# Loads of small tables issued inside the phase before, and the last projection stores no longer waited for

## Chip, cores and metric

One core of a Trainium2 chip. The metric is the device time of one execution in microseconds; the time before is the median of three runs.

## The reference, cut to what matters

A small network over 256 latent and 256 context tokens of width 1024: two layers with adaptive normalisation (adaln), then a block with a router and 32 experts. Layer 0 mixes neighbourhood attention and a bidirectional mLSTM; layer 1 is an RWKV-7 mixer; block 2 mixes a gated delta rule and a state-space scan. What the change touches is how their small parameters come on chip: norm gains, gate biases, rope and mask tables, the decay tables w2 and a2, the rows k_a and r_k, the router's bias. The computation is not changed.

```python
def modulate(x, shift, scale):
    return rms_norm(x) * (1.0 + scale) + shift
...
    r, k, v = jnp.einsum('sbtd,sde->sbte', jnp.stack([xr, xk, xv]), w_rkv)
    w_logit = w0[:, None, None, :] + jnp.einsum('zbtr,zrd->zbtd', jnp.tanh(jnp.einsum('btd,zdr->zbtr', xw, w1)), w2)
    decay = jnp.exp(-jnp.exp(-jax.nn.softplus(-w_logit.astype(jnp.float32)) - 0.5))
    a = jax.nn.sigmoid(a0[:, None, None, :] + jnp.einsum('zbtr,zrd->zbtd', jnp.einsum('btd,zdr->zbtr', xa, a1), a2))
...
    k_dir = k[None] * (1.0 + (a - 1.0) * k_a)
...
    s = s * wt[:, :, None, :] + sa[..., None] * bt[:, :, None, :] + vt[..., None] * kt[:, :, None, :]
```

## The kernel before

The kernel is a chain of phases. A Phase (from L131) owns semaphores and buffers; at its end it clears the semaphores and puts a barrier over all engines (L157), so no engine begins the next phase before all have ended this one. Inside a phase each engine has its own program, and they meet on semaphores.

Weights come through a ring of three slots of 2 MB (class Ring). SP issues a ring load (L219) when the matmuls of the chunk that used the slot are done, and it runs up to three slots ahead, so that the first three weight chunks of the next stage are under way when a phase ends. All of SP's loads go through one queue, the ring's and the small ones; ScalarE's stores of the projection go through another.

Small tables come through load (L3375), a phase of its own: SP issues all loads of the list (L3384), waits for all of them, and the barrier follows. There are nine such phases: ldx (const 1280 KB, x 4 x 512 KB) at the very start; ldab (gate_b, qn, kn, rope; 328 KB) between norm0a and the projection of layer 0; ldsel (sel 8 KB, head_row 256 KB) before mlstm_rows; ldrw (w2 512, a2 512, masks 673, ka 512, rk 512 KB) between rw_project and the scan rw_chunks; ldro (v 2 x 512, lnx_w 512, lnx_b 512, g2 512 and 128 KB) between gate_rows and rw_readout; ldgain (8 KB) between adaln and norm_T of block 2; ldconv (taps 72, cbias 18, small2 32 KB) before gd_conv; ldmix (gn 64, sn 512 KB) before gd_merge; ldmoe (router_b 16, iota 512 KB) before the router.

Phases that the change touches:
- adaln (L416): twelve chunks of 2 MB of ada_w through the ring, each multiplied by the silu of the condition (L481), copied out by ScalarE (L450), turned (L470) and added to the bias on VectorE (L461).
- gate_rows (L489): VectorE spreads gate columns (L503), TensorE turns them (L517), VectorE copies them out (L507).
- norm_T (L522): squares on ScalarE (L550), scale on VectorE (L561), normalised rows (L572), turned by TensorE (L586), written to xT by VectorE (L542).
- mlstm_rows (L1028): scans over gate rows on VectorE alone.
- rw_project (L1410): 20 units of k, v, r; VectorE copies each to one of three stage buffers, ScalarE stores it to a scratch tensor in HBM (L1570). At the end ScalarE waits for all stores, those of k times k_k (kk) too.
- rw_chunks (L1676): eight steps of a scan; SP loads k, kk, r (L1735) and v (L1740) for each; the first matmuls are logits (L1774 with the bias rows, L1775 with w2 and a2); mix_k (L2117) uses ka, k and kk; bonus uses rk from the third step on.
- gd_merge (L2780), where VectorE uses gn and sn after a root by ScalarE.

Of the kernel before, what the change touches and what calls it, by code (L numbers as in the profile page):

```python
# [13 lines left out]
ALU = mybir.AluOpType  # L14
# [3 lines left out]
P = 128  # L18
# [219 lines left out]

class G:
# [176 lines left out]
def adaln(g, name, cond, bias, mod):  # L416
# [3 lines left out]
    with Phase(g, name) as ph:  # L420
# [33 lines left out]

# [34 lines left out]
def gate_rows(g, name, cols, rows):  # L489
# [3 lines left out]
    with Phase(g, name) as ph:  # L493
# [3 lines left out]
        with nc.Block() as block:  # L497
            @block.vector
# [23 lines left out]
def norm_T(g, name, tiles, dst, scale, shift, gain=None, off=0):  # L522
# [4 lines left out]
    with Phase(g, name) as ph:  # L527
# [8 lines left out]
        with nc.Block() as block:  # L536
            def drain(dve, i):
# [490 lines left out]
def mlstm_rows(g, rowg, rowo, cols):  # L1028
# [4 lines left out]
    with Phase(g, "mlrows") as ph:  # L1033
# [4 lines left out]
        with nc.Block() as block:  # L1038
            @block.vector
# [370 lines left out]
def rw_project(g, mu, krow, lora_w, bias_rows, scr, low_w, low_a, sg0, sg1, b16, pick, loads):  # L1410

    nc, ring = g.nc, g.ring
    DEPTH, BANKS, STAGES = 7, 4, 3
# [5 lines left out]
    with Phase(g, "rwproj") as ph:  # L1419
# [4 lines left out]
        stage = ph.sb("stage", [P, STAGES, 512])  # L1424
        kkb = ph.sb("kk", [P, 2, 512])
# [17 lines left out]
        s_st = [ph.sem(f"stored_{i}") for i in range(STAGES)]  # L1443
# [4 lines left out]
        with nc.Block() as block:  # L1448
# [11 lines left out]
            def _(pool):  # L1460
# [20 lines left out]
                def finish(u):  # L1481
                    pool.wait_ge(s_ri, u + 1)
                    o = kkb[:, u % 2, :]
                    v.tensor_tensor(heads8(o), heads8(o), rep(ss[:, 2, 8 * u:8 * u + 8], RW_D, 2), ALU.mult).then_inc(s_kk, 1)

                for u in range(KK_UNITS):
# [4 lines left out]
                    v.tensor_tensor(kkb[:, u % 2, :], stage[:, u % STAGES, :], krow[:, c * 512:c * 512 + 512], ALU.mult)\  # L1491
# [45 lines left out]
            def _(act):  # L1537
# [5 lines left out]
                def square(u):  # L1543
# [3 lines left out]
                    nc.scalar.activation(sq[:, 0:512], kkb[:, u % 2, :], ACT.Square).then_inc(s_sq, 1)  # L1547
# [128 lines left out]
def rw_chunks(g, scr, low_w, low_a, w2, a2, ctab, b16, pick, rows, y, coef):  # L1676
# [3 lines left out]
    with Phase(g, "rwkv") as ph:  # L1680
# [2035 lines left out]
```

## Time and profile before

| | |
|---|---|
| runs | 3873.45, 3879.27, 3878.82 us; median 3878.82 |
| profiled execution | 3875.51 us, span 3873.7 |
| TensorE busy | 3174.9 us (82%) |
| VectorE / ScalarE / GpSimd busy | 1503.0 / 889.4 / 308.0 us |
| mean granted TensorE clock | 0.905 of full |
| data moved | 684.76 MB, 177 GB/s over the span |
| expert stage | about the last 1100 us, one expert in every 32 us |

Shares over the span say little here, since stages with different limits follow one another. The order of time and the holes between phases are read from the timeline.

### The profile page before, as it was taken

Reading aid. Unit: us, or ns where it says so; the run is one execution under the profiler, and the core shown is the slowest. Engines: PE = TensorE matmul, PEld = TensorE weight load, DVE = VectorE, ACT = ScalarE, POOL = GpSimd, SP = SyncE. Lnnn points to the kernel's source line nnn. Section 1 sums busy time; section 2 is a strip of 40 time slices with the busy share of each in tenths; the row PEclk is TensorE's granted clock in tenths of the full one; section 3 lists DMA queues with packets and bytes.
Section 4 is the critical chain, followed back from the end, with each engine's and each line's share of the span. In section 5 each row is a group of like instructions: output and inputs, shape, how many; then the busy total and the mean of one; then the engine's idle time right before and its main releaser. Section 6 shows DMA issues by size and latency. Waiting matters only on the chain. (4 is left out here: it accounts for less than half of the span.)

```text
span 3873.7 us, 94421 instructions
## 1 busy us (share of the span) xinstructions
PE 3174.9 (82%) x41870; PEld 2301.0 (59%) x41870; DVE 1503.0 (39%) x2488; ACT 889.4 (23%) x1492; POOL 308.0 (8%) x262
## 2 busy tenths in 40 slices
PE   5886579997686888785896794657699999999996
PEld 2674458885364666674883784644356666666663
DVE  0436653332543554555561596552411111111111
ACT  1214222221221434341441352110111111111110
POOL 0011200000120323130000001310000000000000
PEclk8898789998797999997997896878799999999998
DMA  9130012224434010100457340002399999999993
GB/s 361 69 98 13 4 44 87 109 87 184 166 108 160 25 42 20 47 4 30 153 196 304 112 174 1 1 7 95 145 409 410 410 410 411 411 411 411 411 410 123
DMA packets 219571, 684.76 MB, mean 177 GB/s; under 512 B 25200, under 2 KB 50032, under 8 KB 186432
## 3 DMA queue, kind: packets, MB, share of 16 engines
q1 hardware_dynamic: 190720, 652.85, 43.3%
q10 hardware_dynamic: 28608, 28.33, 2.2%
q8 instruction: 194, 3.18, 0.3%
q14 instruction: 49, 0.40, 0.0%
HBM read 660.16 MB, written 20.97 MB: 176 GB/s over the span
## 5 line engine op out<-in xcount | busy, mean ns | idle before, releaser
L3171 PE MATMUL experts_psum_gu<-ring,experts_x 128*32 128x256 f32 x9216 | 507.3, 381 | 16.2 <-ACT experts_x L3215 16.1
L3171 PEld LDWEIGHTS experts_psum_gu<-ring,experts_x 128*32 128x32 f32 x9216 | 296.4, 110 | 217.9 <-ACT experts_x L3215 16.9
L3275 DVE TENSOR_TENSOR experts_gate<-experts_psum_gu,experts_bias 128x768 f32<-128x768 f32 x32 | 30.6, 957 | 863.3 <-PE experts_psum_gu L3171 863.3
L3194 PE MATMUL experts_psum_down<-experts_weights,experts_hiddenT 128*32 128x256 f32 x6144 | 339.1, 380 | 3.8 <-ACT experts_hiddenT L3223 3.8
L3194 PEld LDWEIGHTS experts_psum_down<-experts_weights,experts_hiddenT 128*32 128x32 f32 x6144 | 200.2, 110 | 136.8 <-issue 5.7
L735 PE MATMUL mlp_psum_bank<-mlp_x_high,mlp_w_high 128*128 128x512 f32 (+1 forms) x512 | 175.5, 343 | 13.4 <-DVE xT_rounded L313 13.4
L287 DVE TENSOR_TENSOR ring_rounded<-ring,mlp_w_high 128x1024 fp32r<-128x1024 f32 x128 | 156.7, 1226 | 50.4 <-ACT mlp_w_high L282 50.4
L735 PE MATMUL mlp_psum_bank<-xT_rounded,mlp_w_high 128*128 128x512 f32 (+1 forms) x512 | 174.8, 342 | 0.0
L735 PE MATMUL mlp_psum_bank<-mlp_x_high,ring_rounded 128*128 128x512 f32 (+1 forms) x512 | 173.7, 339 | 0.0
L3171 PE MATMUL experts_psum_gu<-xT,experts_x 128*32 128x256 f32 x3072 | 171.6, 379 | 0.0
L481 PE MATMUL ada_psum_row<-ring,ada_silu 128*32 128x512 f32 x576 | 99.9, 832 | 84.5 <-DMA ring<-in_ada_w 60.6
L3219 ACT ACTIVATE experts_sigmoid<-experts_gate 128x768 f32<-128x768 f32 x32 | 27.0, 843 | 613.5 <-DVE experts_gate L3277 613.5
L1752 POOL TENSOR_TENSOR rwkv_Lo<-rwkv_L,chunk_masks 128x512 f32<-128x512 f32 x80 | 117.0, 1477 | 461.4 <-DVE rwkv_L L2180 356.2
L3171 PEld LDWEIGHTS experts_psum_gu<-xT,experts_x 128*32 128x32 f32 x3072 | 99.5, 110 | 66.3
L282 ACT CAST mlp_w_high<-ring 128x1024 fp32r<-128x1024 f32 x128 | 133.1, 1042 | 23.1 <-PEq L157 23.1
L749 PE MATMUL mlp_psum_bank<-mlp_w_high,mlp_hidden_high 128*128 128x512 f32 x384 | 118.5, 390 | 1.2 <-ACT mlp_relu L685 1.2
L749 PE MATMUL mlp_psum_bank<-mlp_w_high,mlp_hidden_rounded 128*128 128x512 f32 x384 | 118.3, 389 | 0.0
L749 PE MATMUL mlp_psum_bank<-ring_rounded,mlp_hidden_high 128*128 128x512 f32 x384 | 118.2, 389 | 0.0
L735 PEld LDWEIGHTS mlp_psum_bank<-mlp_x_high,mlp_w_high 128*128 128x128 f32 x512 | 97.7, 191 | 26.2 <-issue 14.2
L368 PE MATMUL projAB_psum_bank<-projAB_w_high,projAB_x_high 128*128 128x512 f32 (+1 forms) x256 | 95.0, 371 | 16.5 <-DVE ring_rounded L287 16.5
L735 PEld LDWEIGHTS mlp_psum_bank<-mlp_x_high,ring_rounded 128*128 128x128 f32 x512 | 97.7, 191 | 12.3
L735 PEld LDWEIGHTS mlp_psum_bank<-xT_rounded,mlp_w_high 128*128 128x128 f32 x512 | 97.7, 191 | 10.9
(646 smaller groups left out, 5893.2 us busy)
## 6 DMA issues: line engine op xcount, KB each, us to landing
ring<-in_w_gu SPq DMA_DIRECT2D x186, 1024.0 KB, 14.5
experts_weights<-in_w_down SPq DMA_DIRECT2D x128, 1024.0 KB, 15.9
ring<-in_ada_w SPq DMA_DIRECT2D x36, 2048.0 KB, 11.9
ring<-in_mlp_w SPq DMA_DIRECT2D x32, 2048.0 KB, 8.2
xT<-in_w_gu SPq DMA_DIRECT2D x64, 1024.0 KB, 15.2
ring<-in_w_in SPq DMA_DIRECT2D x12, 2048.0 KB, 7.5
ring<-in_ab_w_in SPq DMA_DIRECT2D x6, 2048.0 KB, 9.6
ring<-in_w_rkv SPq DMA_DIRECT2D x6, 2048.0 KB, 10.8
```

Source lines behind the costliest of these rows:

```text
L282: self.g.nc.scalar.copy(h, w).then_inc(self.s_high, 1)
L287: self.g.nc.vector.tensor_tensor(low, w, h.bitcast(F32), ALU.subtract).then_inc(self.s_low, 1)
L368: mm = nc.tensor.matmul(banks[:, n % 8, 0:w], a, b[:, kt % 2, :], start=(kt + k == 0), stop=(kt == KT - 1 and k == 2))
L481: mm = nc.tensor.matmul(pr[32 * j:32 * j + 32, n % 4, :], sc[:, kt, :], wv[:, kt, :], start=(kt < GROUPS), stop=(kt >= KT - GROUPS))
L735: mm = nc.tensor.matmul(banks[:, f % 8, 0:n_tok], w[:, kt, :], x, start=(kt + k == 0), stop=(kt == KT - 1 and k == 2))
L749: mm = nc.tensor.matmul(banks[:, 2 * t + c, :], h, w[:, 0, c * 512:c * 512 + 512], start=(f + k == 0), stop=(f == FT - 1 and k == 2))
L1752: v.tensor_tensor(Lo[l][:, :, :], L[l][:, :, :], rep(small(C2_LVL + HALF_LEVELS * d + k), M8), ALU.mult).then_inc(s_lo[l], 1)
L3171: mm = nc.tensor.matmul(pg[o, q, gr, :], x, w[:, c:c + C], start=(u == 0 and gr != 1), stop=(u == U - 1), skip_group_check=True)
L3194: mm = nc.tensor.matmul(pd[o, gr, :], hidT[:, ch, gr, GROUP * v:GROUP * v + GROUP], w[:, ch, C * c:C * c + C], start=(v == 0 and ch == 0 a ...
L3219: nc.scalar.activation(sg[:, :, :], gt[:, :, :], ACT.Sigmoid, scale=SWI_ALPHA).then_inc(s_sg, 1)
L3275: v.tensor_tensor(gt[:, :, :], pg[:, 0, 0:GROUPS, :], rep(bias[:, 0, :], GROUPS), ALU.add).then_inc(s_bg, 1)
```

## The change

A new class Fetch holds a list of loads with a semaphore of its own; issue and wait can stand in different places. Six of the nine load phases become a Fetch that SP issues at the start of a compute phase and waits for at its end: ldab in norm0a, ldsel in mlstm_rows, ldro in gate_rows, ldgain in adaln, ldconv in norm2a (ahead of the projection too), ldmoe in norm2m, with gate_rows behind it. ldmix is issued in gd_merge itself, and VectorE waits for it before it uses the rows. ldx is issued in the first adaln: const before the ring, x behind the first three ring slots; VectorE waits for const, SP for x at the end. ldrw becomes five Fetches issued by SP at the start of rw_chunks, in the order w2, a2, masks, ka, and rk after the first v; each engine waits for each table where it first uses it. rw_project no longer waits for the last three stores; their semaphores live on, their stage buffers lie in the tensor y, and SP waits for them before it first loads r. gn moves from ldmix to the loads in norm2a.

The diff, cut to its core:

```diff
+class Fetch:
+
+
+    def __init__(self, g, name, jobs):
+        self.sem = g.nc.alloc_semaphore(f"{name}_loaded")
+        self.jobs = jobs
+
+    def issue(self, eng):
+        for dst, src in self.jobs:
+            eng.dma_start(dst, src).then_inc(self.sem, 16)
+
+    def wait(self, eng):
+        eng.wait_ge(self.sem, 16 * len(self.jobs))
...
             def _(sync):
                 sync.dma_start(c[:, :, :], cond).then_inc(s_in, 16)
                 sync.dma_start(b[:, :], bias).then_inc(s_in, 16)
+                if before is not None:
+                    before.issue(sync)
+                if fetch is not None:
+                    ring.issue(sync, 0)
+                    fetch.issue(sync)
                 ring.issue(sync, 12)
+                if fetch is not None:
+                    fetch.wait(sync)
...
             @block.vector
             def _(dve):
-
+                if before is not None:
+                    before.wait(dve)
                 nc.vector.tensor_reduce(sel[:, :], blk(g, C_ID).rearrange("p (j c) -> p c j", j=GROUPS)[:, 0:2, :],
                                         AX.X, ALU.add).then_inc(s_silu, 1)
...
+            if fetch is not None:
+                @block.sync
+                def _(sync):
+                    fetch.issue(sync)
+                    fetch.wait(sync)
+
             @block.vector
...
-def mlstm_rows(g, rowg, rowo, cols):
+def mlstm_rows(g, rowg, rowo, fetch):
...
+            @block.sync
+            def _(sync):
+                fetch.issue(sync)
+                fetch.wait(sync)
+
...
-        stage = ph.sb("stage", [P, STAGES, 512])
-        kkb = ph.sb("kk", [P, 2, 512])
+        kkb = [ph.sb("kk", [P, 512])[:, :], stage[:, STAGES, :]]
...
-                for i in range(STAGES):
-                    act.wait_ge(s_st[i], 16 * len(range(i, N, STAGES)))
                 for i in range(2):
                     act.wait_ge(s_kst[i], 16 * len(range(i, KK_UNITS, 2)))
                 act.wait_ge(s_lowc, 4)
+                for i in range(STAGES):
+                    act.wait_ge(s_st[i], 16 * len(range(i, N - STAGES, STAGES)))
...
         with nc.Block() as block:
             @block.sync
             def _(sync):
+                for name in ("w2", "a2", "masks", "ka"):
+                    tables[name].issue(sync)
                 for i, (d, t) in enumerate(steps):
                     if i:
                         sync.wait_ge(s_til, i)
                     for q, name in enumerate(("k", "kk", "r")):
                         if name == "r" and not lat(i):
                             continue
+                        if name == "r" and i == 2:
+                            for slot, (s, count) in enumerate(s_stored):
+                                sync.wait_ge(s, 16 * count)
                         sync.dma_start(ldk[:, q, :], scr[name][t - (2 if name == "r" else 0)]).then_inc(s_ldk, 16)
                     if i >= 2:
                         sync.wait_ge(s_g[1], i - 1)
                     if i >= 2 and lat(i - 2):
                         sync.wait_ge(s_y0[1], sum(lat(j) for j in range(i - 1)))
                     sync.dma_start(vs[i % 2], scr["v"][t]).then_inc(s_ldv, 16)
+                    if i == 0:
+                        tables["rk"].issue(sync)
 
             @block.gpsimd
...
                 take = Take(pool)
                 v = nc.gpsimd
+                tables["masks"].wait(pool)
...
+                tables["w2"].wait(pe)
                 logits(0, 0)
+                tables["a2"].wait(pe)
                 logits(0, 1)
+                tables["masks"].wait(pe)
                 totals(0)
...
                     take(s_sa, 2)
                     take(s_ldk, 16 * (3 if lat(i) else 2))
+                    if i == 0:
+                        tables["ka"].wait(dve)
+                        tables["masks"].wait(dve)
                     ch.link(v.scalar_tensor_tensor(out=k, in0=bt[i % 2][:, :], scalar=-1.0, in1=rows["ka"],
...
+                    if i == 2:
+                        tables["rk"].wait(dve)
...
-def gd_merge(g, p2, og, ys, rows, mix):
+def gd_merge(g, p2, og, ys, rows, mix, fetch):
...
+            @block.sync
+            def _(sync):
+                fetch.issue(sync)
...
                 nc.vector.sem_inc(s_ms, 1)
                 dve.wait_ge(s_rt, 1)
+                fetch.wait(dve)
                 ch.link(nc.vector.reciprocal(ss[:, 0, :], ss[:, 2, :]))
...
-    adaln(g, "ada0", a["cond_col"], a["adab_col"][0], g.mod)
+    adaln(g, "ada0", a["cond_col"], a["adab_col"][0], g.mod, const, x_in)
...
-            load(g, "ldab", [(small[:, 0:16], row(a["gate_b"])), (small[:, 16:80], row(a["qn"])),
-                             (small[:, 80:144], row(a["kn"])), (rope[:, :, :, :], a["rope"])])
+            norm_T(g, "norm0a", ALL_TILES, g.xT, lambda t: mod(1, t), lambda t: mod(0, t),
+                   fetch=Fetch(g, "ldab", [(small[:, 0:16], row(a["gate_b"])), (small[:, 16:80], row(a["qn"])),
+                                           (small[:, 80:144], row(a["kn"])), (rope[:, :, :, :], a["rope"])]))
...
-            load(g, "ldsel", [(sel[:, :, :], a["sel"]), (head_row[:, :], row(a["headn"]))])
-            mlstm_rows(g, rowg, rowo, None)
+            mlstm_rows(g, rowg, rowo, Fetch(g, "ldsel", [(sel[:, :, :], a["sel"]), (head_row[:, :], row(a["headn"]))]))
...
-            load(g, "ldrw", [(w2[:, :], a["w2"]), (a2[:, :], a["a2"])]
-                 + [(ctab[:, :], a["chunk_masks"]), (ka[:, :], row(a["k_a"])), (rk[:, :], row(a["r_k"]))])
-            rw_chunks(g, scr, low_w, low_a, w2, a2, ctab, b16, pick, {"ka": ka[:, :], "rk": rk[:, :]}, y, coef)
+            tables = {n: Fetch(g, f"ldrw_{n}", [(dst[:, :], src)]) for n, dst, src in (
+                ("w2", w2, a["w2"]), ("a2", a2, a["a2"]), ("masks", ctab, a["chunk_masks"]), ("ka", ka, row(a["k_a"])),
+                ("rk", rk, row(a["r_k"])))}
+            n_stores = 2 * (TT + TT + 2)
+            rw_chunks(g, scr, low_w, low_a, w2, a2, ctab, b16, pick, {"ka": ka[:, :], "rk": rk[:, :]}, y, coef, tables,
+                      [(s, len(range(i, n_stores, 3))) for i, s in enumerate(s_stored)])
...
-            load(g, "ldro", [(v[:, t, :], scr["v"][2 + t]) for t in range(2)]
-                 + [(lw[:, :], row(a["lnx_w"])), (lb[:, :], row(a["lnx_b"])), (g2a[:, :], a["g2"][0:P, :]),
-                    (g2b[:, :], a["g2"][P:G_LORA, :])])
+            gate_rows(g, "rows1", [lambda kt, j=j: g.mod[:, 8 * j + kt, 0:1] for j in (2, 5)], rows,
+                      Fetch(g, "ldro", [(g2a[:, :], a["g2"][0:P, :]), (g2b[:, :], a["g2"][P:G_LORA, :])]
+                            + [(v[:, t, :], scr["v"][2 + t]) for t in range(2)]
+                            + [(lw[:, :], row(a["lnx_w"])), (lb[:, :], row(a["lnx_b"]))]))
...
-        load(g, "ldgain", [(gains[:, :, :], a["norm_g_col"])])
-        norm_T(g, "norm2a", LAT_TILES, g.xT, lambda t: mod(1, t), lambda t: mod(0, t), gains[:, 0, :], off=2)
+        adaln(g, "ada2", a["cond2_col"], a["adab2_col"], g.mod,
+              fetch=Fetch(g, "ldgain", [(gains[:, :, :], a["norm_g_col"])]))
...
+            norm_T(g, "norm2a", LAT_TILES, g.xT, lambda t: mod(1, t), lambda t: mod(0, t), gains[:, 0, :], off=2,
+                   fetch=Fetch(g, "ldconv", [(taps[:, :, :], a["taps_col"]), (cbias[:, :], a["cbias_col"]),
+                                             (small[:, :], row(a["small2"])), (gn[:, :], row(a["gdn_norm_g"]))]))
...
-                load(g, "ldconv", [(taps[:, :, :], a["taps_col"]), (cbias[:, :], a["cbias_col"]),
-                                   (small[:, :], row(a["small2"]))])
...
-                load(g, "ldmix", [(gn[:, :], row(a["gdn_norm_g"])), (sn[:, :], row(a["ssd_norm_g"]))])
-                gd_merge(g, p2, og, ys, {"gn": gn[:, :], "sn": sn[:, :]}, mix)
+                gd_merge(g, p2, og, ys, {"gn": gn[:, :], "sn": sn[:, :]}, mix, Fetch(g, "ldmix", [(sn[:, :], row(a["ssd_norm_g"]))]))
...
-            load(g, "ldmoe", [(rb[:, :], row(a["router_b"])), (iota[:, :], row(a["iota"]))])
+            norm_T(g, "norm2m", LAT_TILES, g.xT, lambda t: mod(4, t), lambda t: mod(3, t), gains[:, 1, :], off=2,
+                   fetch=Fetch(g, "ldmoe", [(rb[:, :], row(a["router_b"])), (iota[:, :], row(a["iota"]))]))
+            gate_rows(g, "rows3", [lambda kt: g.mod[:, 40 + kt, 0:1]], rows)
...
-    load(g, "ldx", [(g.const[:, :], a["const"])] + [(g.x[:, t, :], xin[t]) for t in range(TT)])
-    if 0 in parts:
-        layer0(g, a)
+    layer0(g, a, Fetch(g, "ldconst", [(g.const[:, :], a["const"])]),
+           Fetch(g, "ldx", [(g.x[:, t, :], xin[t]) for t in range(TT)]))
```

## Rows read from the trace of the kernel before

**Rows 1.** SP's waits over the whole span: us in total, times, longest.

```profile
SPq L3380 <- DMA gains<-in_norm_g_col: 8.4, 1, 8.4
SPq L3380 <- DMA x<-in_x: 8.1, 1, 8.1
```

**Rows 2.** Timeline of VectorE: start, duration, instruction, idle before and releaser.

```profile
83.35 0.79 DVE L561 TENSOR_SCALAR norm0a_scale<-mod 128x8 f32<-128x8 f32 x4 [0.97 <-PEq L157]
...
392.89 0.48 DVE L1042 MEMSET mlrows_one<- 4x512 f32 x1 [5.76 <-PEq L157]
...
1789.49 1.22 DVE L2267 TENSOR_REDUCE rwread_stats<-rw_y 128x16 f32<-128x1024 f32 x1 [12.18 <-PEq L157]
...
2126.54 0.17 DVE L561 TENSOR_SCALAR norm2a_scale<-mod 128x8 f32<-128x8 f32 x1 [10.64 <-PEq L157]
...
2132.90 5.19 DVE L542 TENSOR_SCALAR xT<-norm2a_psum_turned,norm2a_scale,mod 128x128 f32<-128x128 f32 x16 [0.55 <-PE norm2a_psum_turned L586]
```

**Rows 3.** Timeline: last work before and first work after four load phases.

```profile
101.39 2.31 DVE L542 TENSOR_SCALAR xT<-norm0a_psum_turned,norm0a_scale,mod 128x128 f32<-128x128 f32 x7
...
110.31 4.26 ACT L308 CAST projAB_x_high<-xT 128x512 fp32r<-128x512 f32 x8 [20.43 <-PEq L157]
...
2191.85 0.44 DVE L3390 COPY proj<-proj_psum_bank 128x272 f32<-128x272 f32 x1 [2.58 <-PE proj_psum_bank L368]
...
2200.76 0.12 POOL L2316 MEMSET gdconv_padded<- 128x12 f32 x1 [146.23 <-POOLq L157]
...
2556.16 0.69 DVE L2582 TENSOR_TENSOR og<-og,gdn_psum_lane 128x512 f32<-128x512 f32 x1
...
2563.02 1.28 ACT L2793 ACT_TABLE_LOAD   x1 [11.16 <-PEq L157]
...
2683.45 0.69 DVE L507 COPY rows<-rows_psum_rows 128x512 f32<-128x512 f32 x1 [1.01 <-PE rows_psum_rows L517]
...
2689.89 0.95 POOL L2986 MEMSET slot_tokens<- 128x1024 f32 x1 [147.09 <-POOLq L157]
```

**Rows 4.** Stretches: engines' busy time (x instructions), then PEclk, DMA share, GB/s.

```profile
1183.00:1185.40 2.40, 0.32 (x2) 0.00 (x0) 2.32 (x3) 2.40 (x4) 0.00 (x0) 1.00 1.01 387
1185.50:1188.00 2.50, 2.50 (x6) 2.02 (x7) 2.50 (x3) 1.33 (x2) 0.00 (x0) 0.50 0.68 262
1213.00:1214.00 1.00, 0.00 (x0) 0.00 (x0) 0.00 (x0) 0.00 (x0) 0.00 (x0) 0.50 0.21 80
2116.00:2118.00 2.00, 0.00 (x0) 0.00 (x0) 0.00 (x0) 0.00 (x0) 0.00 (x0) 0.83 1.05 410
2124.00:2126.00 2.00, 0.00 (x0) 0.00 (x0) 0.00 (x0) 0.00 (x0) 0.00 (x0) 0.50 0.10 33
2768.00:3870.00 1102.00, 1063.51 (x18704) 632.92 (x18704) 167.97 (x206) 109.95 (x135) 0.00 (x0) 0.98 0.96 383
```

**Rows 5.** Timeline around gate_rows of layer 1 and the loads of ldro.

```profile
1769.46 3.22 DVE L503 TENSOR_SCALAR rows_wide<-const,mod 128x128 f32<-128x128 f32 x16 [1.63 <-PEq L157]
...
1778.19 0.80 SPq L3384 DMA_DIRECT2D v_lat<-rw_v  x2
```

**Rows 6.** Timeline from the end of the projection to the scan's first step.

```profile
1205.42 0.37 SPq L219 DMA_DIRECT2D ring<-in_mlp_w  x1
1206.15 0.33 ACTq L1570 DMA_DIRECT2D rw_r<-rwproj_stage  x1
...
1224.59 0.58 PE L1774 MATMUL rwkv_psum_lane<-rw_bias_parts,rw_pick 96*128 96x512 bf16 x1 [19.20 <-PEq L157]
...
1236.22 1.23 DVE L2117 SCALAR_TENSOR_TENSOR rwkv_K<-rwkv_B,ka 128x1024 f32<-128x1024 f32 x1 [30.10 <-ACT rwkv_B L2032]
```

**Rows 7.** Timeline of the start: loads of x, ring loads, first matmuls.

```profile
2.11 1.03 SPq L3384 DMA_DIRECT2D x<-in_x  x2
...
12.94 47.03 SPq L219 DMA_DIRECT2D ring<-in_ada_w  x11
...
20.71 3.64 PE L481 MATMUL ada_psum_row<-ring,ada_silu 128*32 128x512 f32 x16 [20.71 <-DMA ring<-in_ada_w]
```

More of the change, by code:

```diff
@@ L413, in plan_rows, with adaln @@
         ring.add(wv[:, a:a + 4, :], units)
-def adaln(g, name, cond, bias, mod):
+def adaln(g, name, cond, bias, mod, before=None, fetch=None):
     nc, ring = g.nc, g.ring
@@ L486, in _, with gate_rows @@
                 turn_row(11)
-def gate_rows(g, name, cols, rows):
+def gate_rows(g, name, cols, rows, fetch=None):
     nc = g.nc
@@ L519, in _, with norm_T @@
                     mm.then_inc(s_mm, 1)
-def norm_T(g, name, tiles, dst, scale, shift, gain=None, off=0):
+def norm_T(g, name, tiles, dst, scale, shift, gain=None, off=0, fetch=None):
     nc = g.nc
@@ L536, in norm_T @@
         with nc.Block() as block:
+            if fetch is not None:
+                @block.sync
+                def _(sync):
+                    fetch.issue(sync)
+                    fetch.wait(sync)
             def drain(dve, i):
@@ L1038, in mlstm_rows @@
         with nc.Block() as block:
+            @block.sync
+            def _(sync):
+                fetch.issue(sync)
+                fetch.wait(sync)
             @block.vector
@@ L1407, in pe, with rw_project @@
             take(self.s[l]["y_new"])
-def rw_project(g, mu, krow, lora_w, bias_rows, scr, low_w, low_a, sg0, sg1, b16, pick, loads):
+def rw_project(g, mu, krow, lora_w, bias_rows, scr, low_w, low_a, sg0, sg1, b16, pick, loads, s_st, stage):
     nc, ring = g.nc, g.ring
-    DEPTH, BANKS, STAGES = 7, 4, 3
+    DEPTH, BANKS, STAGES = 7, 4, len(s_st)
     PROJ = (("k", 2, ALL_TILES), ("v", 3, ALL_TILES), ("r", 0, LAT_TILES))
@@ L1673, with rw_chunks @@
 DECAY = math.exp(-0.5)
-def rw_chunks(g, scr, low_w, low_a, w2, a2, ctab, b16, pick, rows, y, coef):
+def rw_chunks(g, scr, low_w, low_a, w2, a2, ctab, b16, pick, rows, y, coef, tables, s_stored):
     nc = g.nc
@@ L2788, in gd_merge, with _ @@
         with nc.Block() as block:
+            @block.sync
+            def _(sync):
+                fetch.issue(sync)
             @block.scalar
@@ L3395, in row, with layer0 @@
     return ap.partition_broadcast(P)
-def layer0(g, a):
+def layer0(g, a, const, x_in):
     nc = g.nc
-    adaln(g, "ada0", a["cond_col"], a["adab_col"][0], g.mod)
+    adaln(g, "ada0", a["cond_col"], a["adab_col"][0], g.mod, const, x_in)
     mod = lambda j, t: g.mod[:, 8 * j:8 * j + 8, 0 if t >= 2 else 1]
-    norm_T(g, "norm0a", ALL_TILES, g.xT, lambda t: mod(1, t), lambda t: mod(0, t))
     with ExitStack() as outer:
@@ L3491, in layer1 @@
         pick = osb("rw_pick", [96, 4, P], BF16)
+        y = osb("rw_y", [P, 2, D])
+        s_stored = [nc.alloc_semaphore(f"rw_stored_{i}") for i in range(3)]
         with ExitStack() as inner:
@@ L3535, in block2 @@
     nc = g.nc
-    adaln(g, "ada2", a["cond2_col"], a["adab2_col"], g.mod)
     mod = lambda j, t: g.mod[:, 8 * j:8 * j + 8, 0]
@@ L3554, in block2 @@
                 feat = isb("feat", [P, 36, 256])
-                taps = isb("taps", [P, 36, 4])
-                cbias = isb("cbias", [P, 36])
-                small = isb("small2", [P, 64])
                 beta = isb("beta", [P, 2, 8])
@@ L3590, in block2 @@
                 gemm_rows(g, "mixout", 4, mixT, rows[:, 0, :])
-        norm_T(g, "norm2m", LAT_TILES, g.xT, lambda t: mod(4, t), lambda t: mod(3, t), gains[:, 1, :], off=2)
         acc = osb("moe_acc", [P, 2, D])
```

20 lines of the change are left out of this document (10 added, 10 removed).

## Prediction

> **What bounds the kernel now.** I read SP's own waits first. The function load (L3375) is a phase of its own: SP issues a few small loads, waits for all of them, and every other engine stands at the barrier. Nine such waits end on a load, 49.8 us in all; the longest is that for gains (8.4 us), the next that for const and x at the start (8.1) [rows 1]. The wait is only part of what a load phase costs: issue, landing and a second barrier come with it. So I took the whole hole from the timeline, from the last work before a load phase to the first work after it. The kernel is one chain of phases with a barrier between any two, so a hole lies wholly on the path that sets the end. An ordinary phase boundary is still there afterwards. It shows as 0.97 us of idle VectorE between two phases of adaln and norm_T [rows 2], and I leave that much in every hole.
>
> **Seven holes with a long enough cover.** Each is its length less 0.97.
> - ldab: 101.39 + 2.31 = 103.70 to 110.31 is 6.6, so 5.6. ldconv: 2192.29 to 2200.76 is 8.5, so 7.5. ldmix: 2556.85 to 2563.02 is 6.2, so 5.2. ldmoe: 2684.14 to 2689.89 is 5.75, so 4.8 [rows 3].
> - ldsel: VectorE idle 5.76, so 4.8. ldgain: 10.64, so 9.7 [rows 2].
> Sum of these six: 37.6 us. The seventh, ldro, has a short cover and stands below.
>
> What hides the moved loads: ldab goes under norm0a, 83.35 to 103.70 [rows 2, 3]; ldmoe under norm2m, ldsel under the scans of mlstm_rows that start at 392.89, and gains under adaln's 12 chunks. ldmix is not waited for at the end of its phase but by VectorE, behind its own sums and a square root. If a cover were gone, the hole would come back at its old length at most. The tightest of the six is ldconv, now four loads (72, 18, 32 and 64 KB) issued at the start of norm2a. That phase lasts from 2126.54 to 2132.90 + 5.19 = 2138.09, 11.6 us [rows 2]. It will start at about 2116.9, when the ring prefetch still holds the DMA engines: 410 GB/s at 2116 to 2118, and the last data at about 2124.2 [rows 4]. Everything SP issues stands behind it. Before, the step after the last data took from 2124.2 to 2126.54; less the boundary that is some 1.5 us from last data to a released wait. 186 KB at 410 GB/s add 0.5. So the four land near 2126.2, and norm2a has its own work until 2116.9 + 11.6 = 2128.5: 2.3 us to spare. Nothing lost; at worst I give back 3.
>
> **ldro under gate_rows.** Before: gate_rows started at 1769.46, and the five kinds of load (six DMAs, 2688 KB) were issued from 1778.19, with the next phase at work at 1789.49 [rows 2, 5]. From first issue to next work is 11.3 us. The same bytes now start with gate_rows: 1769.46 + 11.3 = 1780.8. The gate_rows work itself ends earlier (1789.49 - 12.18 = 1777.3), so a rest of the wait remains there. Gain 1789.49 - 1780.8 = 8.7. Bounds: 11.2 if they were fully hidden (12.18 - 0.97), 7 if they land 1.7 later. I take the duration that the same loads had. The Trainium skill, page DMA: Bandwidth & Descriptors, section Anatomy of one DMA, fits 2.0 us plus bytes by 436 GB/s for one DMA of the GpSimd path. For 2.75 MB that is an estimate of 8.3 us, a landing at 1777.8, a gain of nearly 11 and a whole sum of 60.5 instead of 58.3. The trace's 11.3 includes issue of six DMAs one behind the other and the boundary, and I go by it.
>
> **The stores of the projection and ldrw.** The last ring load of the phase was issued at 1205.42, the last store of rw_r at 1206.15; the scan's first matmul started at 1224.59 [rows 6]. Between them lie the landing of that store, two boundaries and the load phase of five tables. Now ScalarE doesn't wait for the last three stores, and the scan phase opens near 1207. But w2, the first table, stands on SP's queue behind the 2 MB ring load, whose data ran until about 1213.2 [rows 4]. Its own 512 KB take 1.3 us at 410 GB/s, and 1.5 to release: 1216.0. Gain 1224.59 - 1216.0 = 8.6. Removing the store's wait alone thus buys little more than what the ring load takes back. Next: a2 is needed after the first logits, 5.8 us on, and comes 1.3 after w2. mix_k used ka, k and kk 11.6 us after the first matmul (1236.22 against 1224.59), so at 1227.6. The bytes ahead of the end of kk (w2, a2, 673 KB of masks, ka, k, kk: 3.3 MB) need 8.1 us after 1213.2, so they are there at 1222.8. Nothing late, with 4.8 to spare. rk and the wait of SP for the stores fall two steps later, long after. Bounds: 7, and 13.8 if the ring load were no obstacle.
>
> **The start.** Before: x was issued by 2.11 + 1.03 = 3.14 and landed 8.1 later, at 11.2 [rows 1, 7]. Only then came the first ring load, at 12.94, and the first matmul at 20.71 [rows 7]. Now const and the first ring slot (1.3 + 2.1 MB) are about the bytes that const and x were, behind two more issues (0.5 us each, by the two in 1.03). So the first slot lands near 12.2, 8.5 us earlier. But x, 2.1 MB, now stands between the third and the fourth ring slot, and at 410 GB/s [rows 4] costs 5.1 in a stage that is paced by ring loads to its end. Gain 8.5 - 5.1 = 3.4; bounds 2.5 and 5.
>
> **Sum.** 37.6 + 8.7 + 8.6 + 3.4 = 58.3 us. The profiled execution took 3875.51, which gives 3817.2; the median of the runs is 3878.82, 3.3 above it, which gives 3820.5. I say 3819. The rest (buffers at other addresses, kk in two pieces, gate_rows moved past the allocations) changes no instruction. The expert stage, 1102 us at 383 GB/s and bound by its own loads [rows 4], starts earlier as a whole; nothing in it waits for anything moved.
>
> **Rivals.**
> - *The covers are too short*: the moved loads land later than by my account, above all ldconv in norm2a and ldro in gate_rows, and a phase waits at its end for SP. Price: ldconv 3, ldro 1.7, tables of the scan 1.6, start 1: some 8 to 9 back, 3828. For it: small rows, and the ring load in front. Against: the same queue drained within 2 us of its last data before.
> - *More comes back*: PE rests less and starts at full clock after some of the closed holes. A start at the lower clock costs at least half of 2.5 us [rows 4], say 1.6. Against it: a gap of 2.4 us in the projection with PE at 0.32 busy was followed by a granted clock of 0.50 of full, that is the lower of the two levels, for the next 2.5 us [rows 4], so the remaining gaps of 4 to 10 us will start cold too. Price: three gemm starts at 1.6, and ldro hidden for 2: 7 more, 3812.
> - *The other side*: less rest lowers the granted clock in the long stretches of PE. PE is busy 3174.9 us, 1063.5 of it in the expert stage that is paced by DMA [rows 4], so 2111 count. 58.3 / 2111 = 2.8%: the mean granted clock would have to fall by that from 0.905 to turn the gain into a loss; at 4% it would cost 84 and give about 3905. Nothing speaks for it: the busy expert stage holds 0.98, and low values go with idle slices.
> - *It doesn't do what it says*: the loads stay on the path and only the nine extra boundaries go, 9 x 0.97 = 8.7, so 3870. Against: the issues lie ahead of the work in program order.
>
> **How the numbers follow.** Forecast 0.72, short covers 0.12, more back 0.12, doesn't do it 0.02, clock 0.01, something unnamed 0.01. Low bound of the gain: 4 holes 19.4, ldgain 9.0, ldconv 4.5, ldro 7, scan 7, start 2.5, sum 49.4. High: 20.9 + 9.9 + 7.7 + 11.2 + 13.8 + 5 = 68.5. From 3879 that is 3810 to 3830, and a scatter of the runs of about 3 makes it 3808 to 3833, which also takes in both neighbouring rivals. About 0.2% (8 us) is what a measurement of this kernel can tell from no change; every case but the last three lies far beyond it.
>
> **What would show it.** In the profile after: no row of L3384 and no wait on L3380; VectorE's idle before norm2a, mlrows_one and the conv near 1 us; 3 to 4 us left before rwread; the scan's first matmul 9 to 10 us after the last store; the first matmul of all near 12 us and a break of about 5 us more at the fourth ring slot. Wrong would be: SP released last in norm2a or in the scan, a wait of mix_k for a load, another mean clock.

## The result and the profile after

The kernel before took 3876.14 us (median of 4 runs beside the changed one, 3871.33 to 3879.27), the changed kernel 3816.36 us (median of 4, 3810.66 to 3826.02). The ratio is 0.9849, interval 0.9826 to 0.9873. The difference of the medians is 59.8 us; 58.3 was forecast. The profiled execution of the changed kernel took 3810.66 us with a span of 3808.8, 64.9 less than the span before, and its mean granted clock was 0.911 (0.905 before).

First SP's waits that end on a load, over the whole span. Columns: microseconds in total, times, longest.

```profile
SPq L520 <- DMA lb<-in_lnx_b: 7.6, 1, 7.6
SPq L565 <- DMA gn<-in_gdn_norm_g: 7.2, 1, 7.2
...
SPq L1073 <- DMA head_row<-in_headn: 3.0, 1, 3.0
```

The waits did not vanish. They moved: L565 is the wait at the end of norm_T (for gn, rope and iota, 7.2, 7.0 and 3.3 us), L1073 that of mlstm_rows, L520 that of gate_rows. The waits of the load function [rows 1] are gone. Whether a wait costs something now is not to be seen here. It is to be seen in the timeline, at the first instruction of the next phase. This is that timeline, several engines together (start, duration, instruction, idle before and releaser):

```profile
2.11 6.95 SPq L219 DMA_DIRECT2D ring<-in_ada_w  x3
9.10 5.57 SPq L248 DMA_DIRECT2D x<-in_ctx  x2
...
12.59 3.64 PE L504 MATMUL ada_psum_row<-ring,ada_silu 128*32 128x512 f32 x16 [12.59 <-DMA ring<-in_ada_w]
...
32.88 3.64 PE L504 MATMUL ada_psum_row<-ring,ada_silu 128*32 128x512 f32 x16 [7.24 <-DMA ring<-in_ada_w]
...
80.26 0.79 DVE L596 TENSOR_SCALAR norm0a_scale<-mod 128x8 f32<-128x8 f32 x4 [0.97 <-PEq L157]
...
95.43 5.18 DVE L577 TENSOR_SCALAR xT<-norm0a_psum_turned,norm0a_scale,mod 128x128 f32<-128x128 f32 x16
...
101.54 2.70 ACT L323 CAST projAB_x_high<-xT 128x512 fp32r<-128x512 f32 x5 [14.75 <-PEq L157]
...
378.74 0.48 DVE L1082 MEMSET mlrows_one<- 4x512 f32 x1 [1.28 <-PEq L157]
...
1187.37 0.37 SPq L219 DMA_DIRECT2D ring<-in_mlp_w  x1
1187.38 0.69 DVE L1684 COPY rw_y<-rwproj_psum_bank 128x512 f32<-128x512 f32 x1 [4.88 <-PE rwproj_psum_bank L1570]
...
1190.15 0.35 SPq L248 DMA_DIRECT2D w<-in_w  x1
...
1197.78 0.61 PE L1820 MATMUL rwkv_psum_lane<-rw_bias_parts,rw_pick 96*128 96x512 bf16 x1 [10.44 <-DMA w<-in_w]
...
1209.51 1.22 DVE L2169 SCALAR_TENSOR_TENSOR rwkv_K<-rwkv_B,ka 128x1024 f32<-128x1024 f32 x1 [21.44 <-ACT rwkv_B L2081]
...
1741.69 3.23 DVE L532 TENSOR_SCALAR rows_wide<-const,mod 128x128 f32<-128x128 f32 x16 [1.62 <-PEq L157]
...
1752.85 1.22 DVE L2321 TENSOR_REDUCE rwread_stats<-rw_y 128x16 f32<-128x1024 f32 x1 [4.66 <-PEq L157]
...
2080.41 0.17 DVE L596 TENSOR_SCALAR norm2a_scale<-mod 128x8 f32<-128x8 f32 x1 [0.94 <-PEq L157]
...
2083.67 0.59 SPq L248 DMA_DIRECT2D gn<-in_gdn_norm_g  x1
...
2086.77 5.19 DVE L577 TENSOR_SCALAR xT<-norm2a_psum_turned,norm2a_scale,mod 128x128 f32<-128x128 f32 x16 [0.55 <-PE norm2a_psum_turned L621]
...
2146.07 0.44 DVE L3449 COPY proj<-proj_psum_bank 128x272 f32<-128x272 f32 x1 [2.56 <-PE proj_psum_bank L383]
2147.26 0.12 POOL L2370 MEMSET gdconv_padded<- 128x12 f32 x1 [127.69 <-POOLq L157]
...
2498.45 0.69 DVE L2636 TENSOR_TENSOR og<-og,gdn_psum_lane 128x512 f32<-128x512 f32 x1
...
2500.29 1.28 ACT L2851 ACT_TABLE_LOAD   x1 [6.13 <-PEq L157]
...
2621.41 0.69 DVE L536 COPY rows<-rows_psum_rows 128x512 f32<-128x512 f32 x1 [1.01 <-PE rows_psum_rows L546]
...
2622.98 0.95 POOL L3045 MEMSET slot_tokens<- 128x1024 f32 x1 [137.89 <-POOLq L157]
```

Each hole, read as it was before, against its answer in [rows 2, 3, 5, 6, 7]:

| place | before | after | gain | forecast |
|---|---|---|---|---|
| start (norm0a begins) | 83.35 | 80.26 | 3.1 | 3.4 |
| ldab | 6.6 | 101.54 - 95.43 - 5.18 = 0.93 | 5.7 | 5.6 |
| ldsel | 5.76 | 1.28 | 4.5 | 4.8 |
| stores and scan tables, last ring issue (one moment with the last copy) to first scan matmul | 19.2 | 1197.78 - 1187.37 = 10.4 | 8.8 | 8.6 |
| ldro, end of the scan to readout | 21.7 | 12.8 | 8.9 | 8.7 |
| ldgain | 10.64 | 0.94 | 9.7 | 9.7 |
| ldconv | 8.5 | 2147.26 - 2146.07 - 0.44 = 0.75 | 7.7 | 7.5 |
| ldmix | 6.2 | 2500.29 - 2498.45 - 0.69 = 1.15 | 5.0 | 5.2 |
| ldmoe | 5.75 | 2622.98 - 2621.41 - 0.69 = 0.88 | 4.9 | 4.8 |

The gains add up to 58.3 us. The two spans differ by 64.9, so 6.6 us came from elsewhere. The two largest such pieces are the projection of layer 1 from its first instruction to its last copy (1015.8 to 1205.4 before, 1002.0 to 1187.4 after, 4.2 less; edited there are the place of its buffers and the waits at the end of the phase) and the delta-net scan, where nothing was edited (between turnG and gdmerge, 3.5 less without the hole of ldmix). The first 20 us of that scan as a stretch, before, and then after together with two stretches of edited places. Columns: busy time of PE, PEld, DVE, ACT and POOL with the number of instructions, then PEclk (the granted TensorE clock as a share of full), DMA share, GB/s.

```profile
2426.40:2446.40 20.00, 8.43 (x48) 8.23 (x48) 12.82 (x46) 2.95 (x8) 5.93 (x5) 0.71 0.00 0
```

```profile
2086.00:2088.00 2.00, 2.00 (x11) 2.00 (x10) 1.45 (x5) 0.00 (x0) 0.00 (x0) 0.50 1.05 410
2150.00:2153.00 3.00, 3.00 (x15) 3.00 (x16) 3.00 (x3) 1.29 (x2) 0.00 (x0) 0.50 0.98 378
...
2372.10:2392.10 20.00, 5.62 (x48) 5.43 (x48) 15.47 (x50) 2.88 (x8) 8.78 (x7) 0.79 0.00 0
```

The same 48 matmuls took 8.43 us of PE before and 5.62 after, 2.8 less, at a granted clock of 0.71 and 0.79. Whether the change had to do with that is what the first experiment asks.

### The profile page after: what moved, and what is told of

The parts are those of the page before. It is cut to its first block and busy times, and to the rows that moved or that the text cites. A ratio compares the mean times of both kernels' runs of the same rounds, so it can differ in the third digit from the quotient of the medians.

```text
span 3808.8 us, 94209 instructions
## 1 busy us (share of the span) xinstructions
PE 3161.6 (83%) x41870; PEld 2289.6 (60%) x41870; DVE 1503.5 (39%) x2488; ACT 889.6 (23%) x1492; POOL 310.0 (8%) x262
```

## Experiments

The main theory is the prediction's account: the time that came back is that of the nine places, each with the releaser that the prediction named, and the 6.6 us over it do not belong to the change. Its general rival is that the closed holes speed up the stages behind them as well. Each expectation names the rival that its own run tests. Variants that were run once are read by their holes, since single times of one kernel scatter by more than such an edit is worth.

### The same kernel again

No edit; a second profile and three further runs.

> The changed kernel once more. Theory A (the holes are the whole gain, the rest is the clock's luck): the lengths of the nine places changed agree within 0.3 us with the first profile (first matmul 12.6 us, scan start 10.4 us after the last projection copy, gate_rows' start to readout's start 11.2 us), while three stages without any edit, which were shorter in the first profile of the changed kernel (the gated delta rule by 3.3 us, the projection of layer 1 by 2.7, adaln of block 2 by 1.4), come out at other lengths, spread over 1 to 3 us each, and the span lies some us above 3808.8, near 3815. Rival B (shorter rests speed these stages up): they repeat at their short lengths and the span is 3809 again within 2 us.

Measured: median 3823.18 us (3818.01 to 3826.34), ratio 0.9864, interval 0.9847 to 0.988; span 3818.6, clock 0.911. The interval overlaps that of the first measurement. The holes of ldab, ldsel, ldgain, ldconv, ldmix and ldmoe repeated within 0.02 us, and the scan started 10.6 us after the last copy. From the start of gate_rows to the readout it took 10.7 us instead of 11.2, a little more than the 0.3 that I had allowed. The start did not repeat: norm0a began at 81.87, a gain of 1.5 and not 3.1. The last chunk of adaln and the stretch around it show why, in the first profile and then in the repeat:

```profile
75.19 1.92 PE L504 MATMUL ada_psum_row<-ring,ada_silu 128*32 128x512 f32 x16 [0.89 <-DMA ring<-in_ada_w]
...
75.00:79.00 4.00, 3.80 (x32) 2.28 (x32) 0.00 (x0) 0.58 (x1) 0.00 (x0) 1.00 1.05 409
```

```profile
75.16 3.29 PE L504 MATMUL ada_psum_row<-ring,ada_silu 128*32 128x512 f32 x16 [2.27 <-DMA ring<-in_ada_w]
...
75.00:79.00 4.00, 3.84 (x19) 1.21 (x20) 0.00 (x0) 0.50 (x1) 0.00 (x0) 0.57 1.05 410
```

The last chunk began at the same moment. TensorE had rested 0.89 us in front of it in one execution and 2.27 us in the other, and the clock granted from 75 to 79 was 1.00 and 0.57 of full, so the same 16 matmuls took 1.92 and 3.29 us. Seven profiles have this start (the changed kernel's two, and all experiments below but x behind the ring loads and the combination): the last chunk begins at 75.0 to 75.4 us in all of them, norm0a at 80.1 to 83.8, and in five of the seven at 81.7 or later. So the usual gain of the start is 1.5 to 1.7 us, and 3.1 is one of the best.

Of the three stages that I had named, two repeated their short length: the delta-net scan (135.8 us from turnG to gdmerge in both, 144.3 before, of which 5.0 are the ldmix hole) and the projection of layer 1 (185.4 and 185.5 us, 189.6 before). adaln of block 2 did not (60.2 and 63.0 us, 61.7 before). The span was 9.8 us longer, of which the scan of layer 1 makes 5.5: from its first matmul to the readout it took 560.6 us instead of 555.1, with the same code. So neither theory came true as it was put: A missed on two stages, B on the span. The whole excess over the forecast did not repeat. The two short stages are taken up again where other profiles show their long form.

### The last stores awaited again

```diff
-                    act.wait_ge(s_st[i], 16 * len(range(i, N - STAGES, STAGES)))
+                    act.wait_ge(s_st[i], 16 * len(range(i, N, STAGES)))
```

> ScalarE again waits for the last three projection stores; tables still loaded in order of use. Theory A (the 2 MB ring load in front of w2 takes most of what the removed wait gave): the scan phase opens about 6 us later, but w2 finds the queue nearly empty, lands about 3.7 us after its issue instead of 6.9 or more, and the scan's first matmul comes only 1 to 2 us later against the last copy of the projection (10.4 becomes 11.5 to 12.5). Rival B (the stores' wait was worth its own length): the first matmul comes 6 to 7 us later (about 17).

One run, 3826.49 us. Its timeline at the end of the projection:

```profile
1194.17 0.69 DVE L1684 COPY rw_y<-rwproj_psum_bank 128x512 f32<-128x512 f32 x1 [4.88 <-PE rwproj_psum_bank L1570]
...
1203.25 0.35 SPq L248 DMA_DIRECT2D w<-in_w  x1
...
1206.82 0.61 PE L1820 MATMUL rwkv_psum_lane<-rw_bias_parts,rw_pick 96*128 96x512 bf16 x1 [12.68 <-DMA w<-in_w]
```

From the last copy to the first matmul: 12.65 us, against 10.4 and 10.6 without the wait. The removed wait alone is worth 2.1 to 2.2 us. SP came to w2 at 1203.25, 9.1 after the copy (2.8 in the changed kernel), but w2 then took only 3.6 us until its matmul instead of 7.6, since the ring load had all but drained by then (the trace has it landing at 1203.47). So the two obstacles stand in parallel: removing the stores' wait uncovers the ring load, as the prediction had it.

The projection ahead of that copy took 189.8 us here, as long as in the kernel before (189.6), and 185.3 to 186.3 us in the eight other profiles of the changed kernel and its variants. The restored wait stands behind all of these copies, so it is no cause of their pace that I can name; but the two profiles with the long form are also the two with this wait, and nothing was run that takes them apart.

### The ring load behind the tables

In rw_project, and in rw_chunks behind the issue of rk:

```diff
-                ring.issue(sync, 6)
+                ring.issue(sync, 5)
...
                     if i == 0:
                         tables["rk"].issue(sync)
+                        g.ring.issue(sync, 0)
```

> The ring load of mlp_w1, which stood in front of w2, is issued in the scan's phase behind rk instead. Theory A (w2 waits in the queue): w2 lands 0.9 + 1.3 + 1.5 = 3.7 us after its issue, so the scan's first matmul comes about 4 us earlier, 6.4 us after the last copy instead of 10.4. k and kk then land about 5 us earlier too, no wait of mix_k. Rival B (the landing of w2 is bound by something else, such as its own rows or the stores): still 10 us. The mlp of layer 1 needs the slot 600 us later, so nothing is lost.

One run, 3826.03 us. Timeline at the same place:

```profile
1192.69 0.69 DVE L1684 COPY rw_y<-rwproj_psum_bank 128x512 f32<-128x512 f32 x1 [4.88 <-PE rwproj_psum_bank L1570]
1195.47 0.35 SPq L248 DMA_DIRECT2D w<-in_w  x1
...
1198.88 0.61 PE L1821 MATMUL rwkv_psum_lane<-rw_bias_parts,rw_pick 96*128 96x512 bf16 x1 [6.22 <-DMA w<-in_w]
...
1199.69 0.38 SPq L219 DMA_DIRECT2D ring<-in_mlp_w  x1
```

6.2 us from the last copy to the first matmul, 4.2 less than in the changed kernel, and w2's own way shrank from 7.6 us (1190.15 to 1197.78) to 3.4. The 2 MB ring load, issued 2.8 us ahead of w2, was what w2 waited for. k and kk landed 13.0 and 14.3 us after the last copy instead of 15.9 and 17.5, so about 3 us earlier where I had expected 5; mix_k waited for neither and came 11.7 us after the first matmul, as in the changed kernel. The variant with both, the stores awaited and the ring load behind, was not run. An estimate from the two: w2 issued 9.1 us after the copy and its matmul 3.4 later make 12.5, so with the ring load out of the way the removed wait would be worth 6.3 us and not 2.1.

### x behind the ring loads

```diff
-                    ring.issue(sync, 0)
+                    ring.issue(sync, 9 if before is not None else 0)
```

> x is issued behind all twelve ring slots of the first adaln instead of behind the third. Theory A (x costs its 5.1 us of the DMA engines wherever it stands ahead of the last slot): the break of 7.2 us before the fourth chunk shrinks to about 2, adaln's last row ends near 74.2 instead of 79.3 us, SP then waits for x for about 1 us, and norm0a starts near 76.2 instead of 80.3: 4 us gained. Rival B (the adaln is paced by matmuls and hand-overs, and the break before the fourth chunk is made good later): adaln ends at 78 to 79, and norm0a starts no earlier than 79.

One run, 3823.64 us. Timeline of its start:

```profile
28.11 3.37 PE L504 MATMUL ada_psum_row<-ring,ada_silu 128*32 128x512 f32 x16 [2.25 <-DMA ring<-in_ada_w]
...
72.24 4.69 SPq L219 DMA_DIRECT2D ring<-in_ab_w_in  x1
...
74.10 0.26 DVE L484 TENSOR_TENSOR mod<-ada_psum_mod,ada_bias 128x96 f32<-128x96 f32 x1 [66.24 <-PE ada_psum_mod L493]
...
77.87 0.79 DVE L596 TENSOR_SCALAR norm0a_scale<-mod 128x8 f32<-128x8 f32 x4 [3.51 <-PEq L157]
```

The break at the fourth slot fell from 7.24 to 2.25 us, the last chunk began at 70.3 instead of 75.2, and adaln's last operation at 74.10 instead of 79.03, 4.9 sooner: that is the 5.1 that the prediction charged x for. But VectorE then stood 3.51 us at the boundary, not 0.97. It did not stand for x: SP's waits show none for x, and the trace has x landing at 75.3. SP was still issuing the third prefetch of the next stage, from 72.24 to 76.93, where the same issue took 0.37 us in the changed kernel (from 77.18). I had expected a wait of 1 us for x; what took its place is SP's own issue, 2.5 us over a plain boundary. Net 80.26 - 77.87 = 2.4 us, or 4.0 against the 81.9 of the repeat.

### The readout's loads in two parts

gate_rows waits for the two g2 tables alone; the readout waits for v, lw and lb behind its own sums.

```diff
+            ld_g2 = Fetch(g, "ldro_g2", [(g2a[:, :], a["g2"][0:P, :]), (g2b[:, :], a["g2"][P:G_LORA, :])])
+            ld_rest = Fetch(g, "ldro_rest", [(v[:, t, :], scr["v"][2 + t]) for t in range(2)]
+                            + [(lw[:, :], row(a["lnx_w"])), (lb[:, :], row(a["lnx_b"]))])
...
                 dve.wait_ge(s_rt, 1)
+                if rest is not None:
+                    rest.wait(dve)
```

> gate_rows waits only for g2 at its end; v, lnx_w and lnx_b are waited for by VectorE in rw_readout behind its statistics. Theory A (the rest of the wait left in gate_rows is the landing of the last loads): SP is released before VectorE's last copy, the readout starts 1 us after that copy instead of 4.7, so 3.7 us are gained, and VectorE finds v, lnx_w and lnx_b there, since it asks for them 11 us later. Rival B (reading rw_y and the tables at once slows VectorE, or the loads land so late that VectorE waits): part of the 3.7 shows up again in front of the reciprocal's successors.

One run, 3821.77 us. Timeline of VectorE around the boundary:

```profile
1757.01 1.22 DVE L2323 TENSOR_REDUCE rwread_stats<-rw_y 128x16 f32<-128x1024 f32 x1 [0.94 <-PEq L157]
...
1767.96 0.35 DVE L2333 RECIPROCAL rwread_stats<-rwread_stats 128x32 f32<-128x32 f32 x1 [0.30 <-ACT rwread_stats L2314]
```

The idle time fell from 4.66 to 0.94 us, and the wait for the rest, in front of the reciprocal, found its data there: the releaser is ScalarE, 0.30 us. The 3.7 us that remained of ldro were its late bytes, and they can be hidden. (The diff above leaves out the lines that pass the second list on and issue it behind the first.)

### 512 KB more in norm2a

A further load, of data that nothing uses, ahead of the four small ones:

```diff
-                   fetch=Fetch(g, "ldconv", [(taps[:, :, :], a["taps_col"]), (cbias[:, :], a["cbias_col"]),
+                   fetch=Fetch(g, "ldconv", [(ex[:, :], row(a["ssd_norm_g"])), (taps[:, :, :], a["taps_col"]), (cbias[:, :], a["cbias_col"]),
```

> A load of 512 KB that nobody uses is put in front of the small loads in norm2a. Theory A (all of SP's loads land in the order of the queue, and norm2a hides them by only 0.5 us): the last small load lands 1.3 us later, plus 0.5 for the issue, so SP is released last, VectorE's end to the next phase grows from 0.9 to 1.7 to 2.3 us. Rival B (small loads don't stand behind earlier ones, or the landing is bound by their count): the boundary stays at 0.9.

One run, 3823.08 us. The extra buffer, allocated around this phase, is left out of the diff. Its timeline at the end of norm2a, then its stretch at the start of the delta-net scan:

```profile
2085.88 0.17 DVE L596 TENSOR_SCALAR norm2a_scale<-mod 128x8 f32<-128x8 f32 x1 [0.95 <-PEq L157]
...
2089.77 0.60 SPq L248 DMA_DIRECT2D gn<-in_gdn_norm_g  x1
...
2092.24 5.20 DVE L577 TENSOR_SCALAR xT<-norm2a_psum_turned,norm2a_scale,mod 128x128 f32<-128x128 f32 x16 [0.55 <-PE norm2a_psum_turned L621]
...
2099.10 1.02 ACT L323 CAST ys_rounded<-xT 128x256 fp32r<-128x256 f32 x3 [9.06 <-PEq L157]
```

```profile
2377.30:2397.30 20.00, 8.42 (x48) 8.23 (x48) 12.94 (x46) 2.87 (x8) 6.14 (x5) 0.71 0.00 0
```

The last small load was released at 2089.77 + 0.60 + 7.9 (SP's wait) = 2098.27, 12.4 us into the phase, and VectorE had ended at 2097.44. The boundary grew from 0.92 (next work at 2092.88 in the changed kernel) to 1.66 us, as expected. In the changed kernel the release came at 2083.67 + 0.59 + 7.2 = 2091.46 and VectorE's end at 2086.77 + 5.19 = 2091.96. The spare time was 0.5 us, not 2.3. In the repeat it was 3.4 (2098.1 against 2101.54). There 4.3 us lay between SP's last ring load and the first small load, not 2.6, and SP got that first one out in 0.34 us where the changed kernel's first profile needed 2.06.

The last row is a by-product. The delta-net scan is the same code here as in the changed kernel, and its first 48 matmuls took 8.42 us at 0.71, as in the kernel before. Its whole length was 139.1 us, and 138.5 in ring_behind, with all nine holes closed in both. So closed holes are not enough for the short form.

### Gains and conv loads back in phases of their own

```diff
-        adaln(g, "ada2", a["cond2_col"], a["adab2_col"], g.mod,
-              fetch=Fetch(g, "ldgain", [(gains[:, :, :], a["norm_g_col"])]))
+        adaln(g, "ada2", a["cond2_col"], a["adab2_col"], g.mod)
+        load(g, "ldgain", [(gains[:, :, :], a["norm_g_col"])])
...
+                load(g, "ldconv", [(taps[:, :, :], a["taps_col"]), (cbias[:, :], a["cbias_col"]),
+                                   (small[:, :], row(a["small2"])), (gn[:, :], row(a["gdn_norm_g"]))])
```

> The loads of gains and of the conv (with gn) are load phases again; all else as in the changed kernel. Theory A (the terms add up): the two holes come back, 9.7 and 7.5 us, so the median is 17 us above the changed kernel's, near 3833, ratio to the kernel before 0.989. Rival B (part of a hole was other stages' slack and comes for free): under 12 us.

Median of 4 runs 3844.23 us (3838.66 to 3847.84), ratio 0.9905 to the kernel before, interval 0.9889 to 0.9921, which takes in the 0.989 that was expected. SP's waits and the timeline:

```profile
SPq L3439 <- DMA gains<-in_norm_g_col: 8.3, 1, 8.3
...
SPq L3439 <- DMA gn<-in_gdn_norm_g: 5.2, 1, 5.2
```

```profile
2100.91 0.17 DVE L596 TENSOR_SCALAR norm2a_scale<-mod 128x8 f32<-128x8 f32 x1 [12.24 <-PEq L157]
...
2166.56 0.44 DVE L3449 COPY proj<-proj_psum_bank 128x272 f32<-128x272 f32 x1 [2.56 <-PE proj_psum_bank L383]
...
2175.74 0.12 POOL L2370 MEMSET gdconv_padded<- 128x12 f32 x1 [147.26 <-POOLq L157]
```

Both holes are back: 12.24 us, and 2175.74 - 2166.56 - 0.44 = 8.7. Over the 0.94 and 0.75 of the changed kernel that is 19.3 us. In times: 3879.75, the median of the kernel before measured beside it, less 3844.23 leaves a gain of 35.5, against 59.8 and 54.8 in the two measurements of the changed kernel, so the undoing cost 19.3 to 24.3. The trace's sum lies at the lower end. The expectation was 17; the gains hole was 1.6 longer than in the kernel before. Rival B, under 12 us, is out: these two holes are worth their full length.

### All three: x_last, ring_behind and readout_split together

> x behind all slots of the first adaln, the ring load behind the scan's tables, and the split wait of the readout together. Theory A (the three are independent terms of 4.1, 4.0 and 3.7): 11.8 us under the changed kernel, about 3804 against its median of 3816, ratio to the kernel before 0.9815. Rival B (they disturb one another or a later stage gives them back): 3808 or more.

Median of 5 runs 3813.61 us (3804.13 to 3821.87), ratio 0.9834, interval 0.982 to 0.9847; span of its profile 3802.3, clock 0.911. Two rows of its timeline:

```profile
77.83 0.79 DVE L598 TENSOR_SCALAR norm0a_scale<-mod 128x8 f32<-128x8 f32 x4 [2.16 <-PEq L157]
...
1745.78 1.22 DVE L2324 TENSOR_REDUCE rwread_stats<-rw_y 128x16 f32<-128x1024 f32 x1 [0.94 <-PEq L157]
```

The pieces are all there (the scan started 6.3 us after the last copy; SP was again in the issue of its last prefetch, until 76.9, when adaln had ended). By their single holes they are worth 2.4 + 4.2 + 3.7 = 10.3 us over the changed kernel. The times give 66.1 us under the kernel before measured beside it, where the changed kernel had 59.8 and 54.8, so 6.3 to 11.3 more. That agrees with the sum, but the interval overlaps that of the changed kernel's first measurement, so that it is faster than the changed kernel is likely and not shown by the times. I had expected 3804, 9.6 lower, and a ratio of 0.9815, which lies just outside the interval; by its number alone rival B (3808 or more) was met. Part of that is the start, 2.4 instead of 4.1. For the rest, the 3816 that I had counted from is the lower of two measurements: the repeat of the changed kernel lay 6.8 above it. Whether the three pieces disturb one another is not settled by these times; their holes do not show it.

## Why the prediction was right

**Which holes, and how deep.** Each of the six closed to a plain phase boundary: 0.75 to 1.28 us is left where I left 0.97. ldsel kept 1.28, so it gave 4.5 and not 4.8; ldmix kept 1.15. Both are errors of 0.2 to 0.3. That the sum of nine came out as forecast to the tenth is luck: with the start of the repeat (1.5 instead of 3.1) it is 56.7.

**ldro.** The 11.3 us from first issue to next work, taken over from before, are now 1752.85 - 1741.69 = 11.2, in another phase. The 8.3 us that I estimated from the Trainium skill (page DMA: Bandwidth & Descriptors, section Anatomy of one DMA) would have ended the wait some 2 us sooner: from first issue to release it took 10.3. That page's fit is for one DMA of the GpSimd path, and these are six from SP; the trace disagrees with my use of it, and the measurement decides. Six issues of 0.33 to 0.43 us one behind the other, and 7.6 us from the last of them to its release, are what the sum is made of. Of VectorE's idle time I had 1780.8 - 1777.3 = 3.5 us left, and it was 4.66, 3.7 over a plain boundary. The end of the wait was right; gate_rows' own work was shorter than I took it to be, 6.5 us instead of 7.85. For the same reason my upper bound of 11.2 for this hole was too low: with the wait split, gate_rows to readout took 7.2 us, a gain of 12.8.

**Stores and scan tables.** w2 behind the 2 MB ring load, right in place and size: 1216.0 - 1205.42 = 10.6 us forecast, 10.4 and 10.6 in the changed kernel's two profiles. Two experiments take it apart: the store's wait gives 2.1 to 2.2 given the ring load in front, and the ring load takes 4.2. Without the ring load in front the whole gain is 19.2 - 6.2 = 13.0, near the upper bound of 13.8. mix_k came 1209.51 - 1197.78 = 11.7 us after the first matmul, 11.6 before: nothing late behind it, and kk had landed 4.7 us ahead (4.8 forecast).

**The start: too high in most executions.** First matmul at 12.59 (forecast 12.2), a break of 7.24 at the fourth slot, net 3.1 and in the repeat 1.5 (forecast 3.4, bounds 2.5 and 5). The charge for x, 5.1, was measured at 4.9. What I had left out is the clock behind the last chunk, full in one execution and near half in the next; in five of seven profiles the gain was 1.7 or less, under my lower bound.

**Spare time in norm2a: mis-sized.** The step "the four land near 2126.2 ... 2.3 us to spare" had the right mechanism, since nothing was lost, but the size was wrong: 0.5 in one profile and 3.4 in the other. The step that was off is where the ring prefetch ends against the start of norm2a, taken over from the trace of before, and SP's issues (3.9 us for the four in the first profile) were not in the sum; in the new kernel that prefetch shifts against the phase from execution to execution. The cover held both times, in one by little.

**The rivals.** *Covers too short*: not here; the run with 512 KB more shows what it would look like. (The prices that I listed for it add up to 7.3, not to 8 or 9.) *More comes back*: the first profile looked like it (3810.66, forecast for it 3812), the repeat did not (span 3818.6). The edited starts are cold as forecast: PEclk is 0.50 at 2086 to 2088 and at 2150 to 2153. The delta-net scan is quicker in some profiles by some 3 us, with its matmuls at another clock, but the same code showed both lengths among the variants of the changed kernel (135.8 to 139.9 us from turnG to gdmerge; 139.3 before without the hole), and so did the projection of layer 1 (185.3 to 189.8; 189.6 before). I have one profile of the kernel before, so whether it too shows the short forms now and then stays open, and so does what sets them. The times leave little room for more: gains of 59.8 and 54.8 us against holes of 58.3 and some 57. *Clock lower*: it rose, 0.911 against 0.905, and that needs no faster stage. The closed holes had stood at a granted clock of 0.50 (ldab) to 0.78 (ldmoe), the start at 1.00, by my estimate 0.63 on the whole; 58.3 us of that taken out of 3873.7 us at 0.905 leave 0.909. *Does not do it*: no.

## What to carry to other kernels

A small load in a phase of its own costs issue, landing and a second barrier: 5.8 to 10.6 us each here. Put under the phase before, on its own semaphore, it left at most 0.3 us over a plain boundary at six of six places with enough work above it (0.5 us to spare at the tightest), and 3.7 us where the phase above it had 6.5 us of work and the loads were 2.7 MB. Read the gain as hole less one plain boundary, and look at what stands ahead on the same queue: a 2 MB prefetch in front of the first table that is needed took back 4.2 us, and a wait for stores that is removed is worth only what the next obstacle leaves of it (2.1 here). Look too at how long the issuing engine itself stands in its issues: in x_last that, and not the data, held the phase boundary for 2.5 us. Where one phase needs only part of a fetch at its start, split the wait, not the issue.

## What was not expected of the hardware

SP itself stood in its issues at the start: three ring loads took 6.95 us to issue and the next two, the first of x, 5.57, in the timeline above, while such an issue takes 0.3 to 0.5 us elsewhere. Nearly all of it lies in two single issues, the third ring load's (5.8 us) and the first of x (5.0). As I read it, a load that follows several large ones is not issued until they have moved on. In the changed kernel this cost nothing: the trace has the third slot landing at 22.7 us, x at 24.0 to 27.8 and the fourth slot at 32.8, one right behind the other. In x_last and in the combined kernel it cost about 2.5 and 1.2 us, since SP stood in such an issue when adaln had ended.

The repeat measurements of one kernel differed by 6.8 us in the median (3816.36 and 3823.18), and its single runs by up to 15.7. A part of that is whole stages: the same instructions from the first matmul of the scan of layer 1 to the readout took 555.1 and 560.6 us in two profiles with the same mean clock of 0.911. At the end of the first adaln the clock shows it in small: 1.00 or 0.57 over the same 4 us, and 1.6 us between the two ends.
